# Border sums by GpSimd, second root directly behind the first, and a later split of the second weight unit

## The reference

```python
# first network, a layer
x = x + g1 * heads_out(att_x, px, hy, w_out[l])
x = x + g2 * sq_relu_mlp(modulate(rms_norm(x, norm2_g[l]), sh2, sc2), w_mlp1[l], w_mlp2[l])
...
return rms_norm(x, final_norm_g)
# second network, a layer
u = rms_norm_2(h, norm_g[layer, 0]) * (1.0 + sc1) + sh1
y = ...  # hgrn2_mixer in layer 0, dilated_attention_mixer in layer 1
h = h + (1.0 + g1) * rms_norm_2(y, norm_g[layer, 1])
u = rms_norm_2(h, norm_g[layer, 2]) * (1.0 + sc2) + sh2
y = swiglu_ffn(u, ffn_w_in[layer], ffn_w_out[layer])
h = h + (1.0 + g2) * rms_norm_2(y, norm_g[layer, 3])
```

## Time and profile before

| | us |
|---|---|
| median of 3 runs | 3851.92 |
| lowest and highest | 3847.77, 3854.98 |
| profiled execution, its own time | 3851.2 |
| its span, first to last instruction | 3849.4 |
| TensorE busy | 3546.0 (92%) |
| VectorE busy | 1979.5 (51%) |
| ScalarE busy | 1365.0 (35%) |
| GpSimd busy | 4.6 (0%) |

### The profile page before, as it was taken

How to read it: one execution, slowest core, us unless ns; L and a number is a source line. 1 busy time by engine, 2 the same in 40 slices (tenths; PEclk the granted TensorE clock), 3 DMA queues, 4 the chain that set the end, 5 groups by cost and what they waited for, 6 DMA issues and landing times.

```text
span 3849.4 us, 43254 instructions
## 1 busy us (share of the span) xinstructions
PE 3546.0 (92%) x18038; PEld 2888.2 (75%) x18038; DVE 1979.5 (51%) x2741; ACT 1365.0 (35%) x1914; POOL 4.6 (0%) x13
## 2 busy tenths in 40 slices
PE   7899988999999999789997997999879999969997
PEld 3685547888888755588886776888778888768886
DVE  5436446777445454465545556433455545563335
ACT  3322343422323333353345445422443333362223
POOL 0000000000000000000000000000000000000000
PEclk9999998999999999999998998999989999989998
DMA  4331013445443230145532221222222323212221
GB/s 173 131 117 54 11 33 107 135 153 164 132 142 119 79 104 0 44 149 176 183 110 66 55 66 55 88 90 96 77 73 66 93 68 88 65 55 98 89 96 47
DMA packets 366626, 360.68 MB, mean 94 GB/s; under 512 B 65072, under 2 KB 312031, under 8 KB 365024
## 3 DMA queue, kind: packets, MB, share of 16 engines
q1 hardware_dynamic: 366211, 357.84, 30.1%
q10 hardware_dynamic: 220, 0.07, 0.0%
HBM read 350.02 MB, written 4.72 MB: 92 GB/s over the span
## 4 chain that ended last, share of the span: by engine, by line
PE 44%; DVE 6%; ACT 6%; issue 2%; DMA 0%; SPq 0%; DVEq 0%; ACTq 0%
PE ps L402 38%; ACT second_w_hi L472 1%; PE ps L2503 1%; DVE second_w_lo L530 1%; DVE r_st L2397 1%; DVE sums L463 1%; PE ps L2524 1%; ACT second_scr L668 1%; PE ps L2526 1%; PE ps L2276 1%; PE ps L2513 1%; DVE second_scr L852 0%; DVE x_res L854 0%; DVE second_scr L679 0%; DVE sq L460 0%
## 5 line engine op out<-in xcount | busy, mean ns | idle before, releaser
L402 PE MATMUL ps<-second_h_hi,second_w_hi 128*128 128x512 f32 (+1 forms) x2216 | 833.4, 376 | 117.4 <-DVE second_h_lo L880 59.0
L402 PE MATMUL ps<-second_h_lo,second_w_hi 128*128 128x512 f32 (+1 forms) x2216 | 813.8, 367 | 0.0
L402 PE MATMUL ps<-second_h_hi,second_w_lo 128*128 128x512 f32 (+1 forms) x2216 | 813.3, 367 | 0.0
L530 DVE TENSOR_TENSOR second_w_lo<-ring,second_w_hi 128x2048 fp32r<-128x2048 f32 (+2 forms) x176 | 373.2, 2121 | 505.6 <-ACT second_w_hi L472 505.6
L402 PEld LDWEIGHTS ps<-second_h_hi,second_w_hi 128*128 128x128 f32 x2216 | 432.9, 195 | 185.2 <-issue 72.6
L402 PEld LDWEIGHTS ps<-second_h_lo,second_w_hi 128*128 128x128 f32 x2216 | 432.9, 195 | 63.6 <-issue 1.7
L402 PEld LDWEIGHTS ps<-second_h_hi,second_w_lo 128*128 128x128 f32 x2216 | 431.0, 194 | 65.4
L472 ACT ACTIVATE second_w_hi<-ring 128x2048 fp32r<-128x2048 f32 (+2 forms) x176 | 311.4, 1770 | 348.7 <-PE ps L402 337.1
L402 PE MATMUL ps<-h_mix_hi,w_hi 128*128 128x512 f32 (+3 forms) x776 | 276.7, 357 | 27.8 <-DVE h_mix_lo L695 17.7
L402 PE MATMUL ps<-h_mix_lo,w_hi 128*128 128x512 f32 (+3 forms) x776 | 273.1, 352 | 0.0
L402 PE MATMUL ps<-h_mix_hi,w_lo 128*128 128x512 f32 (+3 forms) x776 | 272.5, 351 | 0.0
(11 more groups left out here) (402 smaller groups left out, 5726.6 us busy)
## 6 DMA issues: line engine op xcount, KB each, us to landing
ring<-in_w_mlp SPq DMA_DIRECT2D x64, 1024.0 KB, 5.3
side_w<-in_ada_w SPq DMA_DIRECT2D x96, 512.0 KB, 4.3
ring<-in_ffn_w_in SPq DMA_DIRECT2D x44, 1024.0 KB, 5.1
side_w<-in_w_mod SPq DMA_DIRECT2D x80, 512.0 KB, 3.8
ring<-in_attn_w_in SPq DMA_DIRECT2D x48, 512.0 KB, 5.2
ring<-in_hgrn_w_in SPq DMA_DIRECT2D x32, 512.0 KB, 4.8
ring<-in_ffn_w_out SPq DMA_DIRECT2D x16, 1024.0 KB, 4.9
ring<-in_w_in SPq DMA_DIRECT2D x14, 1024.0 KB, 5.4
```

Of the source, the lines that this page charges most:

```text
L402: mm = pe.matmul(acc, lhsT, rhs, start=k == 0 and wp == ap, stop=k == j.kt - 1 and wp == 1)
L530: dve.tensor_tensor(unit.place(unit.slot[1]), unit.place(M.ring[:, u % RING, :]), unit.place(unit.slot[0]), ALU.subtract).then_inc(*S.w_lo ...
```

## The change

It has four parts.

- **GpSimd adds.** Product and sum of a job in the second network (`add_sums`) are issued on GpSimd and not on DVE, directly behind the job and no longer one job later. At the entry, both additions of squares go to GpSimd for all blocks but the first (`by_pool`). A new queue `gpsimd` walks the job list and waits for nothing but these jobs. For the last border (`gain == 7`) ACT leaves out the square with the gain, and GpSimd the product and two of the three sums, for all blocks but the first; they are not used there.
- **The second root behind the first.** In `BorderThread`, ACT's second root follows the first one without the position `at(2)` between them, the high parts come one position earlier each and one batch a position, and DVE's steps begin one position earlier.
- **One unit ahead.** At a section's beginning, only unit 0 is split before the side threads' first work; the other free slots are filled behind it.
- **Low parts later.** In jobs of the second half of the tokens (`slow`), DVE makes a freed slot's low part one job later, behind the next evacuation.

```diff
--- before.py
+++ after.py
@@ -249,7 +249,7 @@
         self.engine, self.evac, self.kind, self.hidden, self.dst = engine, evac, kind, hidden, dst
         self.needs, self.after, self.weights_first = needs, after, weights_first
 
-        self.square, self.wide, self.sums = square, None, None
+        self.square, self.wide, self.sums, self.by_pool, self.slow = square, None, None, False, False
 
 
 def cut(w, r0, r1, c0, n=UNIT, jobs=()):
@@ -443,24 +443,41 @@
                 act.wait_ge(S["sums_added"].sem, S["sums_added"].at(j.sum_nth - both))
         dst = acc if fresh else self.scratch(j)
         act.activation(dst[:, 0, :], y, ACT.Square)
-        act.activation(dst[:, 2, :], y, ACT.Square, scale=g)
+        if not j.sums_last:
+            act.activation(dst[:, 2, :], y, ACT.Square, scale=g)
         act.activation(y, y, ACT.Identity, scale=g, bias=0.0).then_inc(*S["sums_act"].one)
 
-    def add_sums(self, dve, j):
+    def add_sums(self, pool, j):
 
         S = self.S
         y, x, _, acc, fresh = j.sums
         for sig, n in j.sums_after:
-            dve.wait_ge(sig.sem, sig.at(n))
-        dve.wait_ge(S["sums_act"].sem, S["sums_act"].at(j.sum_nth + 1))
+            pool.wait_ge(sig.sem, sig.at(n))
+        pool.wait_ge(S["sums_act"].sem, S["sums_act"].at(j.sum_nth + 1))
         if fresh:
-            dve.tensor_tensor(acc[:, 1, :], y, x, ALU.mult).then_inc(*S["sums_added"].one)
+            pool.tensor_tensor(acc[:, 1, :], y, x, ALU.mult).then_inc(*S["sums_added"].one)
             return
         dst = self.scratch(j)
-        dve.tensor_tensor(dst[:, 1, :], y, x, ALU.mult).then_inc(*S["sums_dve"].one)
-        dve.wait_ge(S["sums_dve"].sem, S["sums_dve"].at(S["sums_dve"].sent))
-        dve.wait_ge(S["sums_added"].sem, S["sums_added"].at(j.sum_nth))
-        dve.tensor_tensor(acc, acc, dst, ALU.add).then_inc(*S["sums_added"].one)
+        parts = slice(0, 1 if j.sums_last else 3)
+        if not j.sums_last:
+            pool.tensor_tensor(dst[:, 1, :], y, x, ALU.mult).then_inc(*S["sums_product"].one)
+            pool.wait_ge(S["sums_product"].sem, S["sums_product"].at(S["sums_product"].sent))
+        pool.wait_ge(S["sums_added"].sem, S["sums_added"].at(j.sum_nth))
+        pool.tensor_tensor(acc[:, parts, :], acc[:, parts, :], dst[:, parts, :], ALU.add).then_inc(*S["sums_added"].one)
+
+    def gpsimd(self, pool):
+        S, M = self.S, self.M
+        for j in self.jobs:
+            if j.by_pool:
+                n = j.n
+                for done, added, nth, dst, i in ((S.sq_act, S.sq_add, j.square_nth, j.square[1], 0),
+                                                 (S["wide_act"], S["wide_add"], j.wide_nth, j.wide[1], 1)):
+                    pool.wait_ge(done.sem, done.at(nth + 1))
+                    pool.wait_ge(added.sem, added.at(nth))
+                    pool.tensor_tensor(dst, dst, M.sq[:, i, 0:n], ALU.add).then_inc(*added.one)
+            if j.sums:
+                self.add_sums(pool, j)
+        yield 0
 
     def high(self, act, u):
         S, M, unit = self.S, self.M, self.units[u]
@@ -473,11 +490,12 @@
 
     def scalar(self, act):
         S, M = self.S, self.M
-        u = 0
+        u = 1
+        self.high(act, 0)
+        yield -1
         while u < len(self.units) and self.freed(u) < 0:
             self.high(act, u)
             u += 1
-        yield -1
         for j in self.jobs:
             m, n = j.split_nth, j.n
             if j.engine == "act":
@@ -532,11 +550,12 @@
 
     def vector(self, dve):
         S, M = self.S, self.M
-        u, pending = 0, None
+        u = 1
+        self.low(dve, 0)
+        yield -1
         while u < len(self.units) and self.freed(u) < 0:
             self.low(dve, u)
             u += 1
-        yield -1
         for j in self.jobs:
             m, n = j.split_nth, j.n
             if j.engine == "dve":
@@ -550,28 +569,21 @@
                 dve.wait_ge(S.hi.sem, S.hi.at(m + 1))
                 dve.tensor_tensor(j.dst(j.hidden.lo), M.v[:, m % 2, 0:n], j.dst(j.hidden.hi),
                                   ALU.subtract).then_inc(*S.lo.one)
-            if j.square:
+            if j.square and not j.by_pool:
                 _, dst, fresh = j.square
                 dve.wait_ge(S.sq_act.sem, S.sq_act.at(j.square_nth + 1))
                 if fresh:
                     dve.engine_nop().then_inc(*S.sq_add.one)
                 else:
                     dve.tensor_tensor(dst, dst, M.sq[:, 0, 0:n], ALU.add).then_inc(*S.sq_add.one)
-            if j.wide:
+            if j.wide and not j.by_pool:
                 _, dst, fresh, _ = j.wide
                 dve.wait_ge(S["wide_act"].sem, S["wide_act"].at(j.wide_nth + 1))
                 if fresh:
                     dve.engine_nop().then_inc(*S["wide_add"].one)
                 else:
                     dve.tensor_tensor(dst, dst, M.sq[:, 1, 0:n], ALU.add).then_inc(*S["wide_add"].one)
-            if pending:
-                self.add_sums(dve, pending)
-            pending = None
-            if j.sums and j.sums_now:
-                self.add_sums(dve, j)
-            elif j.sums:
-                pending = j
-            while u < len(self.units) and self.freed(u) <= j.at:
+            while u < len(self.units) and self.freed(u) <= j.at - j.slow:
                 self.low(dve, u)
                 u += 1
             yield j.at
@@ -599,6 +611,10 @@
             def _(dve):
                 weave(self.vector(dve), [s.vector(dve) for s in self.sides])
 
+            @block.gpsimd
+            def _(pool):
+                weave(self.gpsimd(pool), [s.gpsimd(pool) for s in self.sides])
+
 
 class NormThread(Thread):
 
@@ -655,10 +671,10 @@
         self.rstd(act, self.SUM_BANK, S["norm_sum"], S["norm_ln"], S["norm_rstd"], self.first)
         yield from self.high_parts(act, 0)
 
-    def high_parts(self, act, step):
+    def high_parts(self, act, step, pace=0.5):
         S, a, b = self.S, self.a, self.b
         for i in range(self.n_batches):
-            yield self.at(step + i // 2)
+            yield self.at(step + int(i * pace))
             ks, scr = self.batch(i)
             at = self.batch0 + i + 1
             act.wait_ge(S["norm_p"].sem, S["norm_p"].at(at))
@@ -820,12 +836,11 @@
         if self.last:
             return
         act.preload_act_table_set("natural_log")
-        yield self.at(2)
         act.wait_ge(S["post_mean"].sem, S["post_mean"].at(n + 1))
         act.activation(t, t, ACT.Ln, scale=1.0 / self.width, bias=M.eps[:, 0:1]).then_inc(*S["post_ln"].one)
         act.wait_ge(S["post_ln"].sem, S["post_ln"].at(n + 1))
         act.activation(t, t, ACT.Exp, scale=-0.5).then_inc(*S["post_rstd"].one)
-        yield from self.high_parts(act, 3)
+        yield from self.high_parts(act, 2, 1)
 
     def mean(self, dve):
 
@@ -860,7 +875,7 @@
 
     def vector(self, dve):
         S, n = self.S, self.post
-        yield self.at(2)
+        yield self.at(1)
         dve.wait_ge(S["norm_rstd"].sem, S["norm_rstd"].at(self.first + 1))
         if self.last:
             for i in range(2):
@@ -870,11 +885,11 @@
         self.residual(dve, 0)
         dve.wait_ge(S["post_rstd"].sem, S["post_rstd"].at(n + 1))
         self.product(dve, 0)
-        yield self.at(3)
+        yield self.at(2)
         self.residual(dve, 1)
         self.product(dve, 1)
         for i in range(self.n_batches):
-            yield self.at(4 + i)
+            yield self.at(3 + i)
             ks, scr = self.batch(i)
             dve.wait_ge(S["norm_hi"].sem, S["norm_hi"].at(self.batch0 + i + 1))
             dve.tensor_tensor(self.split.lo[:, ks, self.a:self.b], scr, self.split.hi[:, ks, self.a:self.b],
@@ -2054,6 +2069,7 @@
 
         for j in squared(js):
             b, (a, e) = j.where
+            j.by_pool = b > 0
             j.wide = (M.x[:, b, a:e], M.wide[:, a:e], b == 0, M.col("final_norm_g", k=b))
         return js
 
@@ -2716,7 +2732,7 @@
         for j in js:
             b, (a, e) = j.where
             j.sums = (M.y[:, b, a:e], M.x[:, b, a:e], M.gain2[:, gain, b:b + 1], M.sums[:, :, a:e], b == 0)
-            j.sums_now = b == KD - 1
+            j.sums_last, j.slow = gain == 7, a > 0
             j.sums_after = [(S["entered"], 2)] if gain == 1 else [(S["post_x"], gain - 1)]
         return js
```

## The result

The changed kernel takes 3815.98 us (median of 4 runs, 3810.63 to 3816.88), the kernel before 3849.9 in the same comparison (3847.77 to 3854.98). The ratio is 0.9907, with a 95% interval of 0.989 to 0.9924: 34 us less, where the prediction said 43. The profiled execution took 3815.58 us, its span is 3813.8.

The account below looks back on a forecast made before the run. PE was taken as the bound, so only its waits pay: 12.6 + 11 + 6 + 12.5 + 7.5 = 49.6 us, less 6.5 for interference, a gain of 43 us to 3808 us; range 3786 to 3830.

Parts of the forecast that it names:

- the first rival: Borders: full interference, VectorE and GpSimd exclude each other, costing 13 us; 36.6 us gained, 3815 us; chance 0.25.
- The other signs: PE's beginning waits shrink, border waits under 5 us, sums waits of 4 us and more, a new second-half wait.
- Beginnings: Section beginnings: PE starts 9.4, 2.2 and 1.9 us earlier, 0.9 given back; 12.6 us gained.
- The beginnings don't pay: Rival at section beginnings: PE waits for unit 1, split later; 12.6 us less gained, 3821 us; chance 0.08.
- GpSimd's pace: Border sums: from the copy's rate, GpSimd takes 0.62 + 1.88 = 2.5 us a block.
- GpSimd the bound: Rival at the borders: GpSimd at 5.0 us a block is slower than PE; 3889 us; chance 0.05.
- GpSimd fast: Rival at the borders: GpSimd adds at the memset's rate, 5 to 9 us more gained each; 3781 us; chance 0.07.
- Interference: VectorE and GpSimd both reading SBUF: cost between 0 and 13 us, half taken, 6.5 us.
- Roots behind each other: Borders 1 to 3: mean follows the first root, shortening PE's waits; 11, 6 and 12.5 us gained.
- A: Moment at which the sums of a half are complete; in border 1 predicted at 2371.8, against 2367.97 before.
- Low parts later: Second halves: evacuations ahead of low splits only reorder VectorE work that PE has already passed; 0 us.
- Last border: Last border: lighter sums, the 4.30 us wait vanishes, 3.28 becomes about 2; 7.5 us gained.

Follow-up runs that it names:

- e4: The changed kernel with the second network's additions back on VectorE, one job late as before; the entry's additions stay on GpSimd: 3798.8 us, ratio 0.9866.
- e3: The kernel before with only the additions moved to GpSimd, last border's cut included; roots, low parts and beginnings as before: 3861.5 us, ratio 1.003.
- e6: The changed kernel with the additions of jobs 512 tokens wide back on VectorE, those of half-width jobs on GpSimd: 3816.6 us, ratio 0.991.
- e5: The changed kernel with VectorE's low parts in the second halves not one job later: 3840.6 us, ratio 0.9971.
- e8: The changed kernel with the second network's additions on VectorE and the weights' low parts in second halves two jobs later, not one: 3793.46 us, ratio 0.9852.
- e11: The changed kernel with additions on VectorE and, in second halves, the weights' low parts behind the border's own step: 3799.22 us, ratio 0.9872.
- e12: The changed kernel with additions on VectorE and, in second halves, the weights' low and high parts behind the border's own step: 3799.6 us, ratio 0.9865.

## Why the prediction was right, and where not

The time was 8 us above the forecast and inside the range, and it fell on the figure of the first rival (3815). By the prediction's own sign (a split of 2.29 us that shows 4 beside a GpSimd sum) that rival is also the one whose mechanism the rows show: 5.24 us. That its sum came so close is in part luck, since the stretches missed it in both directions: 9.8 us ahead of border 1 for its 12.6, 10.3 in border 3 for its 8.1. The other signs came, but for border 2, where 5.20 us of wait are left for "under 5". By its steps:

- **Beginnings, 12.6 us.** The three waits shrank by 9.4, 2.2 and 1.8, as worked out (9.4, 2.2, 1.9). Alone the part brought 11.3. The second section's gain was lost again on the way: PE is 2.8 us ahead at 1345 us and 0.4 behind at 1571, with the same waits in between. The granted clock is lower in the two windows below, 0.91 for 1.00 and 0.83 for 0.91. "The beginnings don't pay" is out.

Windows of 20 us before and after (stretch, length, PE busy, granted clock, DMA share, GB/s; the kernel before with all engines):

```profile
1340.00:1360.00 20.00, 17.05 (x67) 12.23 (x66) 3.46 (x5) 6.48 (x10) 0.00 (x0) 1.00 0.53 185
1400.00:1420.00 20.00, 17.02 (x70) 12.55 (x71) 8.61 (x19) 7.09 (x13) 0.00 (x0) 0.91 0.00 1
```

```profile
1340.00:1360.00 20.00, 17.05 (x56) 0.91 0.71 215
1400.00:1420.00 20.00, 18.10 (x69) 0.83 0.00 1
```

- **GpSimd's pace, 0.62 + 1.88 us a block.** Right: 0.73 + 1.82 alone. The copy's rate was the right neighbour. Of the rivals, "GpSimd the bound" (from 3.8 us) and "GpSimd fast" are out.
- **Interference, half of 13 us.** This step failed, and it was a choice, not a calculation: with the whole 13 the sum gives 3815. The wait for the sums in border 2 grew by 6.1 us (10.37 for 4.30), between the 5.0 without interference and the 7.7 with it; PE meets border 1's first sums 7.3 us later, counted from its first wait there, against 3.9 and 6.6. The two effects that I priced are both in the rows: the split behind the full-width sum (5.24 us) and the collisions of the second halves. e4 and e3 show that the move costs more than that: 17.2 us in the changed kernel by the medians, 15.3 of them from border 1 on, and 14.7 of PE's idle time. How much of it is interference is not shown. I never priced VectorE keeping the additions in the new order, at 1.38 us a block against 2.6 and with nobody to collide with. That would have shown that the change has a better half.
- **Roots behind each other.** The chain came out nearly as walked. The first low part of the activations comes at A + 16.6 by my count, and starts PE at A + 19.4 (2365.41 to 2384.82); 2.3 of the 2.8 us are a low part of 3.60 for 2.29, one of 1.74 for 1.22 and a product of 1.65 for 1.23, all beside GpSimd. The remaining waits were 2.44 and 1.04 for my 1.5 and 2.3, the new wait 6.92 for my 5. Borders: 7.2, 0.3, 10.3 and 8.1 us for 11, 6, 12.5 and 7.5. With 4.4 less in each of the first three, as full interference has it, that is 6.6, 1.6, 8.1 and 7.5. The 2 us for cheaper restarts do not show in border 1, whose stretch has PE busy for 384.2 us before and 385.1 after.
- **Low parts later, 0.** Wrong by the largest amount, though the sum hides it. I walked the order of the changed kernel, so the gain was in the borders' terms; but I put it down to the roots. The runs give this line 14.2 us on VectorE's additions and 24.6 on GpSimd's, of which 13.4 and 15.0 are PE's idle time. "It only reorders work that PE has passed" looked at PE and not at ScalarE, which waits for that evacuation, and for which VectorE then waits.
- **Last border, 7.5 us.** 8.1 measured; the wait of 4.30 is gone, 3.28 became 2.21.

What would be needed to show how much of this is collision and how much GpSimd's own pace was not tried: e6 took away one collision alone and the pace took over at once.

## What to carry to other kernels

Before work is moved to a second engine, price it in the new order on the engine that had it: here the order brought the gain, and the move gave 15 to 17 of 53 us back. Where two engines feed each other, look at what each has queued behind its wait; one job of distance between an evacuation and a split took 13 to 15 us off PE's idle time. And when two prices of an unknown are far apart and a mechanism stands behind one of them, walk both to the end rather than take the middle.

## What the runs showed of the hardware

- A weight split of VectorE and a sum of GpSimd exclude each other for the whole instruction where both read SBUF: 2.29 us became 5.24 behind a sum of 3.42, and with one SBUF input on VectorE 1.23 became 4.18. A copy from PSUM to SBUF is untouched at 0.42 us.
- GpSimd adds two float32 tensors of 128x768 in 1.82 us and 128x1536 in 3.42 when alone, VectorE in 0.96 and 1.76: a factor of 1.9.
- The stretch between the entry of the second network and border 1, which no edit touches, takes PE 301.9 us in the changed kernel and in e4 (2040.19 to 2342.10, 2038.17 to 2340.11), and 305.0 in e5, e6, e8, e11 and e12, with the same waits. From 2200 to 2340 us the granted clock reads 0.98 in the former:

```profile
2200.00:2340.00 140.00, 129.90 (x786) 0.98 0.20 61
```

and 0.95 in the latter, here e8:

```profile
2200.00:2340.00 140.00, 130.56 (x767) 0.95 0.20 61
```

Over the whole stretch both read 0.94. Up to the wait near 2305 us e5 keeps pace with the changed kernel within 0.1 us (2304.60 us less its start of 2038.91, and 2305.81 less 2040.19), and the 3 us come behind it: from 2300 to 2340 the clock reads 1.00 in the changed kernel and in e4, 0.91 in e5, e6 and e8. Why it fell there is not shown.

So a stretch that no edit touched can hide or feign 3 us. e8, e11 and e12 all carry them and e4 does not. Counted from border 1's first wait to the last group's first transpose, the three take 1444.3, 1447.5 and 1446.9 us and e4 1449.0, one execution each.
